# First attention of a two-layer block by pairs of heads: row tiles for the scores, outputs computed turned in column halves, bias and maximum in one instruction

## The chip, the cores and the metric

The kernel runs on one core of a Trainium2 chip. The metric is device time in microseconds (us) for one execution of the whole program, from a batch of 1 x 512 x 1024 activations to the result. Lower is better.

## The reference, cut to what matters

The program computes a first block (a mixing layer, an expert-choice layer, a gated layer) and then a second one (a gated MLP and a dilated attention). The change lies in the mixing layer of the first block: four pooling groups of 128 channels, and a neighbourhood attention of 8 heads of 64 channels over a grid of 8 rows by 64 columns. All rows are in reach; of the columns each query sees 16.

```python
z = rms_norm(x, norm_mix) @ w_in                    # 512 x 2048: u, q, k, v
y_pool = einsum(window_mean_g(u) - u, w_pool[g]) * pool_scale      # g = 0..3, windows 2, 4, 8, 16
q = rms_norm(q, q_norm) * HD ** -0.5;  k = rms_norm(k, k_norm)
s = einsum('bhcd,bhicjd->bhcij', q_r, k_nb) + rpb[:, dr, dc]       # within the column window
o = softmax(s) @ v_nb
x = x + concat([y_pool, o]) @ w_out
```

## The kernel before, in words

The program is written engine by engine, with semaphores, and each engine runs its own list in order. TensorE fills banks of PSUM (eight of them, 512 float32 a partition each); VectorE and ScalarE read them. A list `order`, made by `note`, says in which order TensorE fills banks and which engine frees each; fill number i takes bank i modulo 8, and `begin` waits until the fill eight places earlier has been read.

The projections `q`, `k` (turned, channels on partitions: `Q1`, `K1`, two heads of 64 partitions to a chunk of 128) and `v` (`V1`, tokens on partitions) stand in SBUF when the attention starts. There are 32 items, one for each query tile of 128 tokens and head (`ITEMS1`, head fastest, L337). The two outer query tiles need 256 keys, the two inner ones 384 (`KEYS1`), so there are 16 items of each width. Float32 matmuls are issued as two matmul records each.

For item j, the engines do this (loops at L843 on TensorE, L1236 on ScalarE, L1611 on VectorE):

- TensorE writes the mask of the column window into a bank (L849, bf16, one column wide per key) and adds the scores of one head to it (L850, 64 partitions deep).
- VectorE adds the relative position bias and writes `S1` (L1621), then takes the negated maximum over the row (L1624).
- ScalarE computes the exponential with the row sum (L1252, and a separate instruction that reads the sum).
- TensorE turns the probabilities of item j-2 in 128 x 128 pieces (L857), ScalarE copies them to `PT1` (L1244).
- TensorE multiplies the turned probabilities of item j-3, as the stationary operand, with `V1`, 64 columns wide (L864). VectorE scales the result by the reciprocal of the row sum (L1629, L1634) into `O1`, tokens on partitions.

Between items VectorE does 8 folds of 1 MB weight slabs (L1463, two instructions each) for the second block's modulation, at j = 2, 5, 8, ..., and TensorE sums one of the results at j = 12 (`ada_cols`, L817). GpSimd computes the pooling windows meanwhile (L708 to L722) into `pool_d`.

After the items TensorE does two 512-wide sums (`ada_rows`, L824), the four pooling matmuls (L874), and 16 transposes of `O1` (L879, fills `ot1`). ScalarE and VectorE split pooling results and attention outputs into a high and a low part (`BH`, `BL`; L1215, L1519, L1648), and TensorE starts `w_out` (L796 to L798), which needs chunk after chunk of them (`f_lo`). Then come norm, router, top-k, and 16 experts, whose weights arrive by DMA in a ring of 12 slabs.

Of the kernel before, what the change touches and what calls it, by code (L numbers as in the profile page):

```python
# [7 lines left out]
P = 128  # L8
D = 1024
KD = D // P  # L10
S = 512
# [68 lines left out]
def bass_kernel(nc, a, out):  # L80
# [8 lines left out]
    with ExitStack() as ctx:  # L89
# [31 lines left out]
        ACC1 = at("ada_acc1", 136, [P, D])  # L121
# [5 lines left out]
        DT = at("pool_d", 90, [P, 4, S])  # L127
# [3 lines left out]
        P1 = [at(f"p1_{i}", 105 + 1.5 * i, [P, 384]) for i in range(2)]  # L131
        PT1 = [at(f"pt1_{i}", 108 + 1.5 * i, [P, 384]) for i in range(2)]
        O1 = at("o1", 112 + 8, [P, NT, 512])
# [65 lines left out]
        RS = [st(38), st(39)]  # L199
        RR = [st(40), st(41)]  # L200
# [4 lines left out]
        SSV = st(112, 16)  # L205

# [94 lines left out]

        order, fills, count = [], {}, {"act": 0, "dve": 0, "lo": 0}
        ring0 = [0]

        def note(key, eng):
            count[eng] += 1
            fills[key] = (len(order), eng, count[eng], ring0[0])
            order.append(key)
# [14 lines left out]
        def note_attn(tag, n):  # L323
            for j in range(n + 3):
# [6 lines left out]
                if tag == "a1" and j == 12:  # L331
                    note(("ada", 1), "dve")
# [11 lines left out]
        ITEMS1 = [(t, h) for t in range(NT) for h in range(H1)]  # L344
        note_attn("a1", len(ITEMS1))
# [4 lines left out]
        for c in range(4):  # L350
            note(("ot1", c), "lo")
# [12 lines left out]
        N_BEFORE_E, ring0[0] = len(order), len(order)  # L364
        COUNT_BEFORE_E = dict(count)
        note_norm(2)
# [64 lines left out]
        def bank(key):  # L431
            i, _, _, r0 = fills[key]
            return PS[(i - r0) % 8]
# [26 lines left out]
        a_nm, a_exp, a_rr = sem("neg_max"), sem("exp_done"), sem("row_rec")  # L460
# [90 lines left out]
        def item1(j):  # L551
            tr, h = ITEMS1[j]
            t = NT - 1 - tr
            kts = KEYS1[t]
            return tr, t, h, kts, len(kts) * P
# [122 lines left out]
        def _(pool):  # L678
# [17 lines left out]
            for g in range(4):  # L696
# [22 lines left out]
                nc.gpsimd.tensor_tensor(DT[:, g, :], cur[:, 8:8 + S], CNT[:, :], ALU.mult).then_inc(p_step, 1)  # L719
                n += 1  # L720
                pool.wait_ge(p_step, n)
                nc.gpsimd.tensor_tensor(DT[:, g, :], DT[:, g, :], UP[:, g, 8:8 + S],  # L722
# [7 lines left out]
        def _(pe):  # L730
# [3 lines left out]
            def begin(key):  # L734

                assert order[at_fill[0]] == key, (order[at_fill[0]], key)
                at_fill[0] += 1
                i, _, _, r0 = fills[key]
                if i - r0 >= 8:
                    _, eng, n, _ = fills[order[i - 8]]  # L740
                    pe.wait_ge(freed[eng], n)
                return bank(key)
# [38 lines left out]
            def tm_unit(ws, keys, ah, al, f0=None):  # L781

                banks = []
                for s in range(2):
                    hi, lo = slab_ready(ws[s])
                    for t in range(NT):
# [3 lines left out]
                        for k in range(4):  # L790
                            kc = 4 * s + k
                            if f0 is not None and t == 0:
                                pe.wait_ge(f_lo, f0 + kc + 1)
# [49 lines left out]
            n_items = len(ITEMS1)  # L843
            for j in range(n_items + 3):
                if j < n_items:
                    tr, t, h, kts, n = item1(j)
                    rows = slice((h % 2) * HD1, (h % 2 + 1) * HD1)
                    b = begin(("a1s", j))
                    mm(b[:, 0:n], ident_bf, CW[:, WINC[t]:WINC[t] + n], start=True, stop=False)  # L849
                    mm(b[:, 0:n], Q1[rows, h // 2, tr * P:(tr + 1) * P],  # L850
                       K1[rows, h // 2, kts[0] * P:kts[0] * P + n], start=False, stop=True).then_inc(filled, 1)
                if 2 <= j < n_items + 2:
                    _, _, _, kts, n = item1(j - 2)
                    pe.wait_ge(a_exp, j - 1)
                    b = begin(("a1t", j - 2))
                    for i in range(len(kts)):
# [1070 lines left out]
```

## Time and profile before

| | us |
|---|---|
| median of 3 runs | 2204.75 |
| lowest, highest | 2201.35, 2206.04 |
| profiled execution, its own time | 2205.0 |
| its span in the trace | 2203.2 |
| TensorE busy | 2036.4 (92%) |
| VectorE busy | 926.9 (42%) |
| ScalarE busy | 568.2 (26%) |

The trace counts from the first instruction's start; the execution's time is 1.8 us more than the span. Busy time of TensorE is modelled from pipelined matmuls, so it says that the engine had work, not that it ran at its peak. The clock that TensorE was granted is shown by stretch, as a share of 2.4 GHz: 1.00 is 2.4 GHz and 0.50 is 1.2 GHz.

### The profile page before, as it was taken

What the parts mean: (1) busy time and instruction counts of PE and PEld (TensorE: products, weight loads), DVE (VectorE), ACT (ScalarE), POOL (GpSimd) and SP (SyncE); (2) the same over time, 40 slices, a digit from 0 to 9 for tenths busy, and PEclk for the clock granted to TensorE, in tenths of its full rate; (3) what the DMA queues carried; (4) which work ended last, traced back from release to release, by engine and by line L of the source; (5) the groups of instructions that cost most, each with busy time, mean ns of one, the idle gap of its engine ahead of it and who ended that gap; (6) DMA issues with size and microseconds to landing.
All of it is one profiled execution on the core that took longest, in us unless ns stands there. A gap on an engine that the chain in (4) does not pass through costs nothing.

```text
span 2203.2 us, 24215 instructions
## 1 busy us (share of the span) xinstructions
PE 2036.4 (92%) x9141; PEld 1209.9 (55%) x9141; DVE 926.9 (42%) x1483; ACT 568.2 (26%) x980; POOL 37.7 (2%) x40
## 2 busy tenths in 40 slices
PE   7999979999999999999999888999999998989798
PEld 6756753332222222222222276888888786867687
DVE  4866451111111111111111165366455758696963
ACT  4333341111001001110011134442232544553510
POOL 1050000000000000000000000000000000000000
PEclk9965889999999999999999988999999998989899
DMA  8441249999999999999999933545243122011010
GB/s 264 139 139 39 103 174 404 422 422 422 422 422 422 422 422 422 422 422 422 422 422 422 415 126 119 194 138 179 93 156 115 60 93 77 20 58 58 20 39 39
DMA packets 132041, 528.15 MB, mean 240 GB/s; under 512 B 9862, under 2 KB 55748, under 8 KB 82692
## 3 DMA queue, kind: packets, MB, share of 16 engines
q1 hardware_dynamic: 129348, 520.55, 60.0%
q0 software_dynamic: 1008, 3.52, 0.7%
q10 hardware_dynamic: 1616, 3.15, 0.4%
q8 instruction: 45, 0.74, 0.1%
q14 instruction: 24, 0.20, 0.0%
HBM read 524.95 MB, written 2.23 MB: 239 GB/s over the span
## 4 chain that ended last, share of the span: by engine, by line
PE 55%; DMA 33%; DVE 7%; ACT 2%; issue 1%; SPq 1%; ACTq 0%; DVEq 0%
DMA w_expert<-in_w_gate 16%; DMA w_expert<-in_w_up 15%; PE bank L776 7%; PE bank L777 7%; PE bank L778 7%; PE bank L963 6%; PE bank L796 5%; PE bank L797 5%; PE bank L798 5%; PE bank L850 2%; PE bank L808 1%; PE bank L864 1%; PE bank L973 1%; DMA raw<-in_w_ple_gate 1%; SPq L630 1%
## 5 line engine op out<-in xcount | busy, mean ns | idle before, releaser
L963 PE MATMUL bank<-w_expert,chosen 128*64 128x512 f32 x2048 | 483.7, 602 | 62.5 <-DMA w_expert<-in_w_up 46.2
L963 PEld LDWEIGHTS bank<-w_expert,chosen 128*64 128x64 f32 x2048 | 130.3, 136 | 396.0 <-issue 232.7
L1710 DVE TENSOR_TENSOR x_res<-x_res,bank 128x512 f32<-128x512 f32 x136 | 87.3, 683 | 428.6 <-PE bank L982 408.3
L776 PE MATMUL bank<-act_hi,w_hi 128*128 128x512 f32 x608 | 248.5, 409 | 0.1
L1473 DVE TENSOR_TENSOR w_lo<-raw,w_hi 128x2048 fp32r<-128x2048 f32 x75 | 171.9, 2292 | 167.2 <-ACT w_hi L1180 167.2
L778 PE MATMUL bank<-act_hi,w_lo 128*128 128x512 f32 x608 | 237.6, 391 | 0.0
L777 PE MATMUL bank<-act_lo,w_hi 128*128 128x512 f32 x608 | 237.6, 391 | 0.0
L973 PE MATMUL bank<-w_expert,hidden_t 128*64 128x512 f32 x1024 | 229.9, 596 | 6.0 <-ACT hidden_t L1332 4.6
L1180 ACT CAST w_hi<-raw 128x2048 fp32r<-128x2048 f32 x75 | 142.9, 1905 | 169.4 <-PE bank L798 163.2
L1732 DVE TENSOR_TENSOR hidden_rows<-gate_silu,bank 128x512 f32<-128x512 f32 x32 | 20.6, 684 | 364.5 <-PE bank L963 364.5
L1535 DVE RECIPROCAL full<-full 128x512 f32<-128x512 f32 x38 | 127.3, 3350 | 64.0 <-ACT full L1234 63.9
L973 PEld LDWEIGHTS bank<-w_expert,hidden_t 128*64 128x64 f32 x1024 | 74.6, 137 | 138.8 <-issue 121.1
L776 PEld LDWEIGHTS bank<-act_hi,w_hi 128*128 128x128 f32 x608 | 114.7, 189 | 28.9 <-issue 5.5
L777 PEld LDWEIGHTS bank<-act_lo,w_hi 128*128 128x128 f32 x608 | 114.7, 189 | 28.2 <-issue 5.5
L778 PEld LDWEIGHTS bank<-act_hi,w_lo 128*128 128x128 f32 x608 | 114.5, 188 | 24.3
L796 PE MATMUL bank<-w_hi,mix_hi 128*128 128x512 f32 x256 | 100.4, 392 | 0.0
L798 PE MATMUL bank<-w_hi,mix_lo 128*128 128x512 f32 x256 | 99.7, 389 | 0.0
L797 PE MATMUL bank<-w_lo,mix_hi 128*128 128x512 f32 x256 | 99.6, 389 | 0.0
L1326 ACT ACTIVATE gate_silu<-bank 128x512 f32<-128x512 f32 x32 | 17.4, 594 | 289.2 <-PE bank L963 289.2
L796 PE MATMUL bank<-w_hi,act_hi 128*128 128x512 f32 x224 | 89.1, 398 | 2.2 <-ACT full L1202 2.2
L797 PE MATMUL bank<-w_lo,act_hi 128*128 128x512 f32 x224 | 88.4, 395 | 0.0
L798 PE MATMUL bank<-w_hi,act_lo 128*128 128x512 f32 x224 | 88.1, 393 | 0.0
(255 smaller groups left out, 2450.4 us busy)
## 6 DMA issues: line engine op xcount, KB each, us to landing
w_expert<-in_w_gate SPq DMA_DIRECT2D x128, 1024.0 KB, 24.9
w_expert<-in_w_up SPq DMA_DIRECT2D x128, 1024.0 KB, 26.5
w_expert<-in_w_down SPq DMA_DIRECT2D x128, 1024.0 KB, 26.2
raw<-in_a_w_in SPq DMA_DIRECT2D x24, 1024.0 KB, 5.7
raw<-in_b_w_in SPq DMA_DIRECT2D x16, 1024.0 KB, 5.3
raw<-in_a_ada_w SPq DMA_DIRECT2D x12, 1024.0 KB, 5.2
raw<-in_b_ada_w SPq DMA_DIRECT2D x12, 1024.0 KB, 5.8
raw<-in_kv_ada_w SPq DMA_DIRECT2D x8, 1024.0 KB, 5.2
```

Source lines behind the costliest of these rows:

```text
L776: mm(b[:, :], hi[:, cols], ah[:, kc, :], start=(kc == 0), stop=False)
L777: mm(b[:, :], hi[:, cols], al[:, kc, :], start=False, stop=False)
L778: last = mm(b[:, :], lo[:, cols], ah[:, kc, :], start=False, stop=(kc == KD - 1))
L796: mm(b[:, :], a_hi, hi[:, r], start=(kc == 0), stop=False)
L797: mm(b[:, :], a_hi, lo[:, r], start=False, stop=False)
L798: last = mm(b[:, :], a_lo, hi[:, r], start=False, stop=(kc == KD - 1))
L963: last = mm(PS[b0 + n][HALF[x], :], XE[:, k % 4, HALF[k // 4]], WE[place][:, r], start=(k == 0), stop=(k == KD - 1), skip_group_check=True)
L973: last = mm(PS[4][HALF[x], :], HT[:, 2 * q + k, HALF[half]], WE[place][:, r], start=(i == 0 and k == 0), stop=(i == 7 and k == 1), skip_gr ...
L1180: nc.scalar.copy(WHI[w % 2][:, :], RAW[slot(n)][:, :]).then_inc(hi_ready, 1)
L1473: tt(WLO[w % 2][:, :], RAW[slot(n_of["W"][w])][:, :], WHI[w % 2][:, :].bitcast(F32), ALU.subtract).then_inc(lo_ready, 1)
L1535: nc.vector.reciprocal(r, r).then_inc(h_rec, 1)
L1710: tt(part, part, ps[:, :], ALU.add).then_inc(d_add, 1)
```

## The change

The 32 items become 16 pairs: pair i is one chunk of two heads and one query tile (`ITEMS1`, tile fastest). TensorE opens two banks, writes the mask into each, and then computes the two heads' scores, one from partitions 0 to 63 and one from 64 to 127. The outputs are computed turned: `V1` (64 columns of one head) is the stationary operand and `PT1` (128 columns) the moving one, and the two heads of a pair write the lower and the upper 64 partitions of one bank, which collects all four query tiles of a chunk. The bank then holds what the 16 transposes of `O1` gave, so these and `O1` go. Since a query is now a column of the output, the reciprocal of the row sum is applied before the transposes, by VectorE, to the probabilities (L1662, 256 or 384 wide, in place). Bias, negation and minimum are one instruction of VectorE (`tensor_tensor_reduce`, L1675), which is issued with a second small one that writes the accumulated column; the exponential takes scale -1. Each pair's output column chunk is split into `BH`, `BL` inside the attention loop, at i = 6, 10, 14 and after the loop. The folds lie at i = 1 to 4 and 8 to 11, `ada_cols` at i = 8. Banks are now given by hand: scores 0 to 3, transposes 4 and 5, outputs 6 and 7. The pooling result goes to `u_padded` in place of `pool_d`. `w_out` waits for the pooling chunks only (`f_chunks`), in its first half.

```diff
+        ITEMS1 = [(c, t) for c in range(H1 // 2) for t in range(NT)]
...
+            for i in range(N1 + 2):
+                if i == 8:
                     ada_cols(1, ACC1)
+                if i < N1:
+                    c, tr, t, kts, n = item1(i)
+                    banks = [begin(("a1s", i, x)) for x in range(2)]
+                    for b in banks:
+                        mm(b[:, 0:n], ident_bf, CW[:, WINC[t]:WINC[t] + n], start=True, stop=False)
+                    for x, b in enumerate(banks):
+                        rows = slice(x * HD1, (x + 1) * HD1)
+                        mm(b[:, 0:n], Q1[rows, c, tr * P:(tr + 1) * P],
+                           K1[rows, c, kts[0] * P:kts[0] * P + n], start=False, stop=True).then_inc(filled, 1)
+                if i >= 2:
+                    c, tr, t, kts, n = item1(i - 2)
+                    pe.wait_ge(freed["act"], fills[("a1t", i - 2, 1)][2])
+                    b = begin(("ot1", c), ends_next=False) if tr == 0 else bank(("ot1", c))
+                    for k, kt in enumerate(kts):
+                        for x in range(2):
+                            last = mm(b[x * HD1:(x + 1) * HD1, tr * P:(tr + 1) * P],
+                                      V1[:, kt, (2 * c + x) * HD1:(2 * c + x + 1) * HD1],
+                                      PT1[2 * (i % 2) + x][:, k * P:(k + 1) * P], start=(k == 0), stop=(k == len(kts) - 1),
+                                      skip_group_check=True)
...
+                if 1 <= i <= N1:
+                    c, tr, t, kts, n = item1(i - 1)
+                    for x in range(2):
+                        slot_ = 2 * ((i - 1) % 2) + x
+                        pe.wait_ge(a_nrm, 2 * (i - 1) + x + 1)
+                        b = begin(("a1t", i - 1, x))
+                        for k in range(len(kts)):
+                            last = nc.tensor.transpose(b[:, k * P:(k + 1) * P], P1[slot_][:, k * P:(k + 1) * P], ident)
+                        last.then_inc(filled, 1)
...
-            for c in range(4):
-                b = begin(("ot1", c))
-                for t in range(NT):
-                    last = nc.tensor.transpose(b[:, t * P:(t + 1) * P], O1[:, t, c * P:(c + 1) * P], ident)
-                last.then_inc(filled, 1)
...
+            def attention1():
+                for i in range(N1 + 1):
+                    if i < N1:
+                        n = item1(i)[4]
+                        for x in range(2):
+                            j = 2 * i + x
+                            act.wait_ge(freed["dve"], fills[("a1s", i, x)][2])
+                            if i >= 2:
+                                act.wait_ge(filled, fill_no(("a1t", i - 2, x)))
+                            nc.scalar.activation(P1[j % 4][:, 0:n], S1[x][:, 0:n], ACT.Exp, bias=NM[x], scale=-1.0,
+                                                 accum_out=RS[j % 4]).then_inc(a_exp, 1)
...
+                    if i >= 6 and i % NT == 2:
+                        ot1_hi(i // NT - 1)
...
+            def probabilities(j):
+                n, p = item1(j // 2)[4], P1[j % 4]
+                dve.wait_ge(a_exp, j + 1)
+                nc.vector.reciprocal(RR[j % 4], RS[j % 4]).then_inc(a_rr, 1)
+                dve.wait_ge(a_rr, j + 1)
+                ts(p[:, 0:n], p[:, 0:n], RR[j % 4], None, ALU.mult).then_inc(a_nrm, 1)
+
+            for i in range(N1 + 1):
+                if i == 8:
                     ada_out(1)
+                for x in range(2):
+                    if i < N1:
+                        c, tr, t, kts, n = item1(i)
+                        h = 2 * c + x
+                        b = take(("a1s", i, x))
+                        if i:
+                            dve.wait_ge(a_exp, 2 * (i - 1) + x + 1)
...
+                        nc.vector.tensor_tensor_reduce(
+                            S1[x][:, 0:n].rearrange("p (j k) -> p j k", k=ROWS),
+                            b[:, 0:n].rearrange("p (j k) -> p j k", k=ROWS), bias, -1.0, 3e38, ALU.add, ALU.min, NM[x]
+                            ).then_inc(freed["dve"], 1)
+                    if i >= 1:
+                        probabilities(2 * (i - 1) + x)
+                if i in (1, 2, 3, 4, 8, 9, 10, 11):
+                    fold(len(folded))
+                if i >= 6 and i % NT == 2:
+                    ot1_lo(i // NT - 1)
+            ot1_lo(3)
```

TensorE's list, before, in the middle of the attention, for one item of 256 keys: mask, scores, two transposes, two output matmuls.

```order
L849 MATMUL bank<-const_wins 128x256 [waits bank_read_by_dve]
L850 MATMUL bank<-k_84,q_83 128x256
L857 MATMUL bank<-const_early,p_1_99 128x128 [waits bank_read_by_act,exp_done]
L857 MATMUL bank<-const_early,p_1_99 128x128
L864 MATMUL bank<-v_85,pt_0_100 128x64 [waits bank_read_by_dve,bank_read_by_act]
L864 MATMUL bank<-v_85,pt_0_100 128x64
```

TensorE's list, of the change, for one pair of 256 keys; the outputs belong to the pair two places earlier and the transposes to the one before.

```order
L868 MATMUL bank<-const_wins 128x256 [waits bank_read_by_dve]
L868 MATMUL bank<-const_wins 128x256
L871 MATMUL bank<-k_84,q_83 128x256 x2
L879 MATMUL bank<-pt_0_101,v_85 64x128 [waits bank_read_by_act]
L879 MATMUL bank<-pt_1_102,v_85 64x128
L879 MATMUL bank<-pt_0_101,v_85 64x128
L879 MATMUL bank<-pt_1_102,v_85 64x128
L879 MATMUL bank<-pt_0_101,v_85 64x128
L879 MATMUL bank<-pt_1_102,v_85 64x128
L893 MATMUL bank<-const_early,p_2_99 128x128 [waits bank_read_by_act,probabilities]
L893 MATMUL bank<-const_early,p_2_99 128x128
L893 MATMUL bank<-const_early,p_3_100 128x128 [waits bank_read_by_act,probabilities]
L893 MATMUL bank<-const_early,p_3_100 128x128
```

The transposes used to wait for the exponential; they now wait for `probabilities`, which VectorE signals after its scaling, once for each head.

VectorE's list, before, for one item: bias, maximum, reciprocal and scaling of earlier items.

```order
L1621 TENSOR_TENSOR s_0_96<-bank,bias_master 128x384 [waits exp_done,bank_filled]
L1624 TENSOR_REDUCE stats<-s_0_96 128x1 [waits bank_read_by_dve]
L1629 RECIPROCAL stats<-stats 128x1 [waits bank_read_by_dve,exp_done]
L1634 TENSOR_SCALAR o_102<-bank,stats 128x64 [waits row_rec,bank_filled]
```

VectorE's list, of the change, for one pair (`ISA` is the fused instruction, with its small second one).

```order
L1675 ISA s_0_95,stats<-bank,bias_master 128x384 [waits exp_done,bank_filled]
L1675 ISA stats 128x1
L1660 RECIPROCAL stats<-stats 128x1 [waits exp_done]
L1662 TENSOR_SCALAR p_2_99<-p_2_99,stats 128x384 [waits row_rec]
L1675 ISA s_1_96,stats<-bank,bias_master 128x384 [waits exp_done,bank_filled]
L1675 ISA stats 128x1
L1660 RECIPROCAL stats<-stats 128x1 [waits exp_done]
L1662 TENSOR_SCALAR p_3_100<-p_3_100,stats 128x384 [waits row_rec]
```

The scaling of pair i-1 stands behind the fused instruction of pair i, head by head, and that one waits for the scores of pair i.

## Rows read from the trace of the kernel before

**Rows 1.** The page: busy time of TensorE, and its granted clock in 40 slices.

```profile
PE 2036.4 (92%) x9141; PEld 1209.9 (55%) x9141; DVE 926.9 (42%) x1483; ACT 568.2 (26%) x980; POOL 37.7 (2%) x40
...
PEclk9965889999999999999999988999999998989899
```

**Rows 2.** Stretches: length; busy (and count) of PE, PEld, DVE, ACT, POOL; PEclk, DMA share, GB/s.

```profile
200.00:220.00 20.00, 20.00 (x69) 13.44 (x69) 11.23 (x27) 6.69 (x20) 0.00 (x0) 0.50 0.00 0
...
235.00:240.00 5.00, 5.00 (x26) 3.23 (x25) 3.48 (x7) 2.93 (x5) 0.00 (x0) 1.00 0.11 15
```

**Rows 3.** Waits from 118 to 235 us: total us, times, longest us.

```profile
PE bank L857 <- ACT p L1252: 4.5, 3, 3.2
```

**Rows 4.** Timeline of one item of 256 keys: start us, us, instruction.

```profile
219.29 0.42 PE L849 MATMUL bank<-const_wins 128*128 128x256 bf16 x1
...
219.64 1.22 PE L850 MATMUL bank<-k,q 64*128 64x256 f32 x2
...
220.90 0.60 DVE L1621 TENSOR_TENSOR s<-bank,bias_master 128x256 f32<-128x256 f32 x1 [1.08 <-PE bank L850]
...
222.01 0.42 PE L849 MATMUL bank<-const_wins 128*128 128x256 bf16 x1
```

**Rows 5.** Timeline, the scores of two successive items of 384 keys.

```profile
165.41 1.65 PE L850 MATMUL bank<-k,q 64*128 64x384 f32 x2
...
169.31 1.65 PE L850 MATMUL bank<-k,q 64*128 64x384 f32 x2
```

**Rows 6.** Timeline of the first item, at the granted clock of 1.00.

```profile
118.54 0.27 PE L849 MATMUL bank<-const_wins 128*128 128x256 bf16 x1 [0.88 <-ACT v L1276]
...
118.74 0.70 PE L850 MATMUL bank<-k,q 64*128 64x256 f32 x2
```

**Rows 7.** Groups by line and shape, 118 to 235 us: count, busy us, mean ns, idle before.

```profile
L1463 DVE SCALAR_TENSOR_TENSOR ada_acc<-raw,stats,ada_acc 128x1024 f32<-128x1024 f32 x14 | 21.5, 1533 | 9.3 <-PE bank L850 9.0
...
L1621 DVE TENSOR_TENSOR s<-bank,bias_master 128x384 f32<-128x384 f32 x16 | 13.4, 835 | 6.6 <-PE bank L850 6.6
...
L1621 DVE TENSOR_TENSOR s<-bank,bias_master 128x256 f32<-128x256 f32 x16 | 9.7, 604 | 7.5 <-PE bank L850 7.5
...
L1624 DVE TENSOR_REDUCE stats<-s 128x1 f32<-128x256 f32 x16 | 6.7, 420 | 0.6
...
L1252 ACT ACTIVATION_READ_ACCUMULATOR p<-s,stats 128x1 f32 x32 | 6.0, 186 | 0.0
...
L1629 DVE RECIPROCAL stats<-stats 128x1 f32<-128x1 f32 x32 | 4.9, 154 | 0.2
```

**Rows 8.** Two lines that scale by a column: ns min/median/max, first and last start.

```profile
L1886 DVE TENSOR_SCALAR diag<-const_early,negmax x96: 273/279/289, 2092.9 to 2146.6; 128x128 f32<-128x128 f32 x96
...
L1460 DVE TENSOR_SCALAR ada_acc<-raw,stats x8: 741/748/1166, 25.5 to 1579.3; 128x1024 f32<-128x1024 f32 x8
```

**Rows 9.** Timeline in an expert: column halves (L963), row halves (L982), at clock 1.00.

```profile
735.03 1.13 PE L982 MATMUL bank<-expert_out,sel_gated_t 64*128 64x512 f32 x4
736.09 1.94 PE L963 MATMUL bank<-w_expert,chosen 128*64 128x512 f32 x8
...
739.02 5.37 PE L963 MATMUL bank<-w_expert,chosen 128*64 128x512 f32 x24
```

**Rows 10.** Stretches at the start of a later attention, columns as in rows 2.

```profile
1962.50:1965.00 2.50, 2.50 (x14) 2.50 (x14) 1.98 (x8) 1.75 (x7) 0.00 (x0) 0.50 0.81 286
1965.00:1967.50 2.50, 2.50 (x19) 2.26 (x18) 2.26 (x11) 2.06 (x10) 0.00 (x0) 0.95 0.03 7
```

**Rows 11.** Timeline behind the attention.

```profile
237.88 1.91 PE L879 MATMUL bank<-const_early,o 128*128 128x128 f32 x16
...
239.54 0.48 PE L796 MATMUL bank<-w_hi,mix_hi 128*128 128x512 f32 x1
...
239.82 3.85 ACT L1215 ACTIVATE mix_hi<-bank 128x512 fp32r<-128x512 f32 x4 [1.05 <-PE bank L879]
...
240.95 4.02 DVE L1648 TENSOR_TENSOR mix_lo<-bank,mix_hi 128x512 fp32r<-128x512 f32 x4 [1.40 <-ACT mix_hi L1215]
```

More of the change, by code:

```diff
@@ L205, in bass_kernel @@
         SSV = st(112, 16)
+        RS = [st(128 + i) for i in range(4)]
+        RR = [st(132 + i) for i in range(4)]
         def pcol(name, k=0, n=1):
@@ L302, in bass_kernel, with note @@
         order, fills, count = [], {}, {"act": 0, "dve": 0, "lo": 0}
-        ring0 = [0]
-        def note(key, eng):
+        ring, holder = [0], {}
+        def note(key, eng, at_bank=None):
             count[eng] += 1
-            fills[key] = (len(order), eng, count[eng], ring0[0])
+            if at_bank is None:
+                at_bank = ring[0]
+                ring[0] = (at_bank + 1) % 8
+            fills[key] = (len(order), eng, count[eng], at_bank, holder.get(at_bank))
+            holder[at_bank] = key
             order.append(key)
@@ L732, in _, with begin, ends @@
             at_fill = [0]
-            def begin(key):
+            def begin(key, ends_next=True):
+                if ends_next:
+                    ends(key)
+                before_ = fills[key][4]
+                if before_ is not None:
+                    pe.wait_ge(freed[fills[before_][1]], fills[before_][2])
+                return bank(key)
+            def ends(key):
                 assert order[at_fill[0]] == key, (order[at_fill[0]], key)
                 at_fill[0] += 1
[L738 to L742, printed above, removed]
             def norm(k):
@@ L791, in tm_unit @@
                             kc = 4 * s + k
-                            if f0 is not None and t == 0:
+                            if f0 is not None and t == 0 and kc < f_chunks:
                                 pe.wait_ge(f_lo, f0 + kc + 1)
@@ new lines, in ot1_lo @@
+            def ot1_lo(c):
+                assert fills[("ot1", c)][2] == f[0] + 1
+                dve.wait_ge(f_hi, f[0] + 1)
+                hi, lo = (x[:, 4 + c, :].rearrange("p (r c) -> p c r", r=ROWS) for x in (BH, BL))
+                tt(lo, from_grid(bank(("ot1", c))[:, :]), hi.bitcast(F32), ALU.subtract).then_inc(f_lo, 1)
+                f[0] += 1
+            def probabilities(j):
[4 more added lines that the diff above has]
+                ts(p[:, 0:n], p[:, 0:n], RR[j % 4], None, ALU.mult).then_inc(a_nrm, 1)
```

133 lines of the change are left out of this document (43 added, 90 removed).

## The prediction

> **What bounds the kernel now.** I read the page first. TensorE has work for 92% of the span, and its granted clock is full nearly everywhere but in the fourth slice, where it is five tenths [rows 1]. The stretches put a place to that: from 200 to 220 us TensorE is busy for all of the 20 us at a clock of 0.50, which is 1.2 GHz, and just behind the attention it is at 1.00 again [rows 2]. So the first attention is bound by TensorE at the lower of its two levels. The waits agree: in the 117 us of the stage TensorE waits 4.5 us for the exponential, in 3 places [rows 3], and the bias, the fold and the output scaling on VectorE wait for TensorE, not the reverse [rows 4, 7]. All that follows (w_out, router, top-k, the experts' weights, whose slabs are asked for as earlier ones are used) starts from the attention's end, so I count a microsecond there as one in the total.
>
> An item of 256 keys takes 222.01 - 219.29 = 2.72 us [rows 4], one of 384 keys 169.31 - 165.41 = 3.90 us [rows 5]. Four pairs of the new kernel (one chunk of two heads, all tiles: two pairs of 256 and two of 384) are eight such items: 4 x 2.72 + 4 x 3.90 = **26.5 us**. There are four such chunks.
>
> **The new loop.** The change puts a ring in place of a pipeline. The transposes of pair i-1 wait for VectorE's scaling of pair i-1, which stands behind the fused instruction of pair i, which waits for the scores of pair i, which stand behind the transposes of pair i-2. One turn of the ring is:
>
> 1. From the first mask to VectorE's first instruction. Before: mask to scores 0.35 us, scores to the bias 220.90 - 219.64 = 1.26 us [rows 4]. Now a second mask is in between, 256 columns at 1.2 GHz, 0.21. Sum 1.82 us. For 384 keys the two masks are 0.11 longer each and the scores (four cycles a column) 0.43: 2.47 us. The second head's scores run on behind and are not waited for.
> 2. Two fused instructions. The trace has none. I take the addition it contains, 0.60 and 0.84 us [rows 7], plus 0.10 for the small second instruction. Bounds: nothing for it, and ScalarE's 0.19 for its own read of a sum [rows 7]; from above also addition plus maximum as now, 0.60 + 0.42. I take the addition because it reads the same bank and the same strided bias. 0.70 and 0.94 each.
> 3. Two reciprocals (0.15 [rows 7]) and two scalings in place. The scaling lies between 0.28 us for 128 columns and 0.75 for 1024 [rows 8]: 0.35 and 0.42 on the line between them. 0.50 and 0.57 together.
> 4. From the last scaling to the next mask: about 0.2 us of signal, the second head's transposes, 2 or 3 of 0.21 us at this clock, 0.1 to the mask: 0.73 and 0.94.
>
> The widths in a chunk run 256, 384, 384, 256. Pair by pair (fused of this pair, scaling and transposes of the one before, lead of the next): 1.4 + 1.0 + 0.73 + 2.47 = 5.6; 1.88 + 1.0 + 0.73 + 2.47 = 6.1; 1.88 + 1.14 + 0.94 + 1.82 = 5.8; 1.4 + 1.14 + 0.94 + 1.82 = 5.3. Sum **22.8 us** against 26.5, and over four chunks **-14.8 us**.
>
> TensorE's own work must fit into that turn. The halves matter here. At 1.2 GHz a pair of 256 keys then needs some 0.56 + 1.28 (scores) + 0.3 (change-over, as between scores and transposes now) + 1.1 to 1.2 (outputs) + 0.95 (transposes) = 4.2 us, one of 384 keys 5.8 us. That is 5.0 on average under a ring of 5.7: TensorE is close behind, and what it saves is not all collected. VectorE's ring is late next.
>
> **Other terms.**
> - Folds: two instructions of 1.28 us, 2.57 us, at eight places. They lie where VectorE otherwise waits for terms 4 and 1 (2.8 to 3.2 us), so the late four cost nothing. While GpSimd pools, they are slower: 14 of them sum to 21.5 us, not 18 [rows 7]. I add **+2**. Were the cover gone (the higher clock), they would cost about 1 us each.
> - The split of a finished output chunk inside the loop: VectorE waits for transposes, ScalarE's copies (about 0.5), ScalarE's high part (3.85 / 4 = 0.96) and then needs 1.0 itself [rows 11]: some 3.6 us after the last scaling, where 2.8 were free. Three times: **+2.5**.
> - Filling and draining with longer turns: **+1**.
> - `ada_cols`: the same 16 small matmuls, moved, not changed: 0. ScalarE does the same exponentials and copies, and scale -1 costs nothing; it has over half its time free [rows 2]. Masks are still one for each head. GpSimd's pooling in place has as many instructions and ends long before it is needed: 0. SP's loads wait for the same folds at the same share of the loop: 0.
> - Behind the attention: the 16 transposes of `O1` go. `w_out` starts at 239.54, and the transposes stood from 237.88 [rows 11]: **-1.65**. The pooling chunks are split by then, or the last within the time of the first matmuls; the attention chunks were split earlier.
>
> Sum: -14.8 + 2 + 2.5 + 1 - 1.65 = **-11 us**. The profiled execution took 2205.0 us, 0.25 over the median of 2204.75, so this gives **2194 us**.
>
> **A rule against the change.** The row first: going from row halves to column halves and back in the experts costs nothing that I can see, 1.06 us for four records being two and a half times 0.43 [rows 9], and I add 0.3 only once in each pair. The Trainium skill (TensorEngine Tiling, Key Properties) says that changing the tiling mode drains the engine. By it a pair would have three such changes (full, rows, columns, full), where two items have four now. If each cost 0.3 us, TensorE's turn would be 4.8 and 6.4 us, 5.6 on average and about the ring's own length, and the total some 2 us higher.
>
> **The rivals.**
> - *The clock comes up.* For it: a later attention starts at 0.50, is busy without a gap, and goes to 0.95 in the next stretch [rows 10]; the new loop has matmul columns flowing for about 79% of a turn where now it is some 72%. Against it: the stage has stayed at 0.50 with TensorE always busy [rows 2], and at the higher clock the same work fills only half of a turn, so that it may fall again. At 1.00 throughout: mask to scores is 0.20 us [rows 6], lead 1.15 and 1.47, term 4 0.51 and 0.62, a chunk 18.4 us, -32.6 for four; folds now stick out, +8; output splits +4.4; +1; `ada_cols` and the 512-wide sums run faster, -3.5; -1.65. Sum -24: **2181 us**; up for half of the time, 2187. [...]
> - *The halves do not overlap here*, since the matmuls are 128 to 384 columns wide and not 512, and each waits for its weights. Then scores cost four records in a row and outputs eight or twelve: 5.3 and 7.6 us a pair, 25.8 a chunk. -2.8 in all, the folds and splits hidden, -1.65: **2200 us**. Rows 9 speak against it.
> - *The fused instruction is slow*, and the change ends slower. It is in the ring twice for each pair, 32 times in all, with nothing to hide it. If it makes a pass for the addition and one as long for the minimum, it takes 1.2 and 1.7 us, 0.6 and 0.8 more than I took: 32 x 0.7 = +22, and **2216 us**. It decides from 11 / 32 = 0.35 us over my price. For it: addition and maximum now take 0.60 and 0.42 us apart [rows 7]. Against: ScalarE's exponential sums in the same pass for 0.19 more.
>
> **How the numbers follow.** Forecast (clock stays at 0.50) 45%, the clock comes up for a part or all 30%, no overlap 15%, slow fused instruction 10%. About 0.2%, 4.4 us, is what a measurement of this kernel can tell from no change. The range runs from the full clock, 2180, to 2203, above the case without overlap with some of the unpriced waits; it leaves out the slow instruction. Faster: the first two and half of the third, 0.82. Same: 0.1. Slower: 0.08.
>
> **What would show it.** In the profile after: the attention ends about 10 us earlier; two successive masks of pairs are 5.3 to 6.1 us apart; TensorE waits before the transposes (L893), for VectorE's scaling; granted clock 0.50; the four score records of 256 keys take 1.3 us and eight output records 1.1 to 1.2 us; the fused instruction 0.6 and 0.84 us. I am wrong on the ring if TensorE does not wait there, on the halves if these records take 1.7 us, on the clock if the stage shows over 0.50.

## The result and the profile after

The changed kernel takes 2179.65 us, median of four runs (2173.96 to 2181.42), beside 2204.96 us for the kernel before on the same chip: a ratio of 0.9893, 95% interval [0.9874, 0.9911]. It is 25 us faster where 11 were forecast, and 0.35 us below the low end of the range. The profiled execution, the slowest of the four, took 2181.42 us, its span is 2179.6 (before: 2203.2, so -23.6 by the trace).

The page of the changed kernel, against [rows 1]:

```profile
PE 1993.5 (91%) x9125; PEld 1175.5 (54%) x9125; DVE 917.6 (42%) x1483; ACT 567.4 (26%) x980; POOL 38.8 (2%) x40
...
PEclk9967999999999999999999998999999998989899
```

TensorE has 43 us less of busy time, of which 24 show in the span: the rest has turned into waits. The fourth slice stands at seven tenths of the clock, where it was five.

Stretches of the changed kernel, with the columns of [rows 2] (length; busy and count of PE, PEld, DVE, ACT, POOL; granted clock, DMA share, GB/s):

```profile
152.65:158.53 5.88, 5.08 (x22) 2.51 (x21) 2.60 (x8) 2.15 (x6) 0.00 (x0) 0.50 0.19 79
...
160.00:180.00 20.00, 17.59 (x90) 10.95 (x88) 13.13 (x34) 6.11 (x19) 0.00 (x0) 0.59 0.16 53
180.00:200.00 20.00, 13.48 (x88) 7.48 (x87) 15.86 (x42) 9.87 (x27) 0.00 (x0) 0.84 0.16 54
...
118.50:205.00 86.50, 64.19 (x322) 35.70 (x322) 65.11 (x141) 35.81 (x93) 29.00 (x23) 0.64 0.31 101
```

TensorE, which was busy for every one of 20 us at 0.50 in [rows 2], is now busy for 64 of 86.5 us and at 0.64 on average. The clock is at 1.00 up to about 125 us, at 0.50 from 126 to 172 us, and goes up and down afterwards.

The waits from 118 to 225 us of the changed kernel (total us, times, longest us), against [rows 3]:

```profile
ACT p L1269 <- DVE stats L1675: 45.8, 31, 5.0
PEld bank L893 <- DVE p L1662: 33.5, 30, 5.2
PE bank L893 <- DVE p L1662: 23.2, 27, 4.6
DVE mix_lo L1654 <- ACT mix_hi L1235: 10.4, 3, 5.5
...
DVE s L1675 <- PE bank L871: 8.7, 5, 3.0
```

This is the ring that the forecast described: before its transposes (L893) TensorE waits for VectorE's scaling in 27 places. VectorE waits for scores in only five; elsewhere a fold or a split mostly fills that time. It also waits three times for ScalarE's part of an output split, but only two of these waits (2.45 us each) lie in the loop. The third stands behind it, and the split at i = 10 finds its input ready, behind a fold:

```profile
160.22 1.05 DVE L1654 TENSOR_TENSOR mix_lo<-bank,mix_hi 128x512 fp32r<-128x512 f32 x1 [2.45 <-ACT mix_hi L1235]
...
184.28 1.01 DVE L1654 TENSOR_TENSOR mix_lo<-bank,mix_hi 128x512 fp32r<-128x512 f32 x1
...
213.03 1.03 DVE L1654 TENSOR_TENSOR mix_lo<-bank,mix_hi 128x512 fp32r<-128x512 f32 x1 [5.54 <-ACT mix_hi L1235]
```

**Where the 23.6 us came from.** Four marks on TensorE, from the timelines:

| mark | before | after | difference, added since the mark above | forecast |
|---|---|---|---|---|
| `ada_rows` begins (attention's end) | 230.67 | 211.85 | -18.8 | -9.3 |
| `w_out` begins | 239.54 | 218.04 | -2.7 | -1.65 |
| first expert matmul | 326.51 | 303.24 | -1.8 | 0 |
| end of the span | 2203.2 | 2179.6 | -0.3 | 0 |

The third row is no work of the change. In the kernel before, the transposes of the router's norm fell into a low clock (0.52 from 289.2 to 292.4 us):

```profile
289.20 3.20 PE L755 MATMUL bank<-const_early,x_norm 128*128 128x128 f32 x14 [0.94 <-DVE x_norm L1492]
```

The same fourteen in the changed kernel, at 1.00:

```profile
268.03 1.75 PE L773 MATMUL bank<-const_early,x_norm 128*128 128x128 f32 x14 [0.94 <-DVE x_norm L1531]
```

1.45 of the 1.8 us are there. From `w_out` to the experts the kernels below take 83.0 to 85.9 us, the kernel before 87.0.

**One turn of the ring, with nothing else in it.** Timeline of the changed kernel from one pair of 384 keys to the next mask (start us, us, instruction):

```profile
152.65 0.84 PE L868 MATMUL bank<-const_wins 128*128 128x384 bf16 x2
...
153.43 1.65 PE L871 MATMUL bank<-k,q 64*128 64x384 f32 x4
155.01 1.12 PE L879 MATMUL bank<-pt,v 128*64 128x128 f32 x8
155.11 0.83 DVE L1675 CUSTOM_DVE_ANT_1 s<-bank,bias_master 128x384 f32<-128x384 f32 x1 [3.00 <-PE bank L871]
155.87 0.08 DVE L1675 DVE_READ_ACCUMULATOR2_ANT stats<- 128x1 f32 x1
155.87 0.16 DVE L1660 RECIPROCAL stats<-stats 128x1 f32<-128x1 f32 x1
...
156.06 0.42 DVE L1662 TENSOR_SCALAR p<-p,stats 128x384 f32<-128x384 f32 x1
156.40 0.84 DVE L1675 CUSTOM_DVE_ANT_1 s<-bank,bias_master 128x384 f32<-128x384 f32 x1
...
157.35 0.42 DVE L1662 TENSOR_SCALAR p<-p,stats 128x384 f32<-128x384 f32 x1
...
157.83 0.90 PE L893 MATMUL bank<-const_early,p 128*128 128x128 f32 x3 [0.39 <-DVE p L1662]
...
158.53 0.64 PE L868 MATMUL bank<-const_wins 128*128 128x256 bf16 x2
```

Mask to VectorE's start: 155.11 - 152.65 = 2.46 us (priced 2.47). The two heads on VectorE: 157.77 - 155.11 = 2.66 us (priced 1.88 + 1.14 = 3.02). Last scaling to the next mask: 158.53 - 157.77 = 0.76 us (priced 0.94). The turn is 5.88 us where the same pieces were priced at 6.43, at the same clock of 0.50. The small second instruction has 0.08 us and begins 0.76 us after its parent's start, at the same moment as the reciprocal: it costs nothing of its own. The signal from the scaling's end to the transposes is 157.83 - 157.77 = 0.06 us, not 0.2.

Groups by line and shape of the changed kernel, 118 to 225 us (count, busy us, mean ns, idle before), against [rows 7]:

```profile
L1502 DVE SCALAR_TENSOR_TENSOR ada_acc<-raw,stats,ada_acc 128x1024 f32<-128x1024 f32 x14 | 22.3, 1592 | 0.3
...
L1675 DVE CUSTOM_DVE_ANT_1 s<-bank,bias_master 128x384 f32<-128x384 f32 x16 | 13.4, 838 | 8.0 <-PE bank L871 7.5 <-ACT p L1269 0.2
...
L1675 DVE CUSTOM_DVE_ANT_1 s<-bank,bias_master 128x256 f32<-128x256 f32 x16 | 9.6, 604 | 1.3 <-PE bank L871 1.2
...
L1662 DVE TENSOR_SCALAR p<-p,stats 128x384 f32<-128x384 f32 x16 | 6.9, 433 | 0.6
L1662 DVE TENSOR_SCALAR p<-p,stats 128x256 f32<-128x256 f32 x16 | 6.8, 426 | 0.6
```

The fused instruction takes 838 and 604 ns, the addition alone took 835 and 604 [rows 7]: the minimum is free. The folds take about as long in all as they did (22.3 us, before 21.5).

**The turns beside each other.** The first masks of five pairs, from TensorE's timeline:

```profile
127.91 0.84 PE L868 MATMUL bank<-const_wins 128*128 128x384 bf16 x2
...
167.42 0.59 PE L868 MATMUL bank<-const_wins 128*128 128x256 bf16 x2
...
192.39 0.49 PE L868 MATMUL bank<-const_wins 128*128 128x384 bf16 x2
...
196.62 0.49 PE L868 MATMUL bank<-const_wins 128*128 128x384 bf16 x2
...
201.71 0.64 PE L868 MATMUL bank<-const_wins 128*128 128x256 bf16 x2
```

The turn from 192.39 to 196.62 took 4.23 us at a clock of 1.00. The one from 196.62 to 201.71 has the same widths as the turn shown above, took 5.09 us where that one took 5.88, and began at the higher clock (0.78 for its first 1.6 us). The six turns from 127.91 to 164.15, where `ada_cols` begins, lie at 0.50 throughout.

### The profile page after: what moved, and what is told of

Read it like the earlier page. It is cut to its first block, busy times and chain, and to the rows that moved or that the text cites. A ratio compares the mean times of both kernels' runs of the same rounds, so it can differ in the third digit from the quotient of the medians.

```text
span 2179.6 us, 24073 instructions
## 1 busy us (share of the span) xinstructions
PE 1993.5 (91%) x9125; PEld 1175.5 (54%) x9125; DVE 917.6 (42%) x1483; ACT 567.4 (26%) x980; POOL 38.8 (2%) x40
## 4 chain that ended last, share of the span: by engine, by line
PE 52%; DMA 33%; DVE 9%; issue 2%; ACT 2%; SPq 1%; DVEq 0%; ACTq 0%
DMA w_expert<-in_w_gate 16%; DMA w_expert<-in_w_up 15%; PE bank L794 7%; PE bank L795 7%; PE bank L796 7%; PE bank L983 6%; PE bank L814 5%; PE bank L816 5%; PE bank L815 5%; PE bank L826 1%; PE bank L993 1%; DMA raw<-in_w_ple_gate 1%; PE bank L1175 1%; DVE s L1675 1%; SPq L643 1%
## 5 line engine op out<-in xcount | busy, mean ns | idle before, releaser
L1365 ACT ACTIVATE gate_silu<-bank 128x512 f32<-128x512 f32 x32 | 17.4, 594 | 289.2 <-PE bank L983 289.2
```

## The experiments

Twelve runs on three chips, each beside the kernel before on its chip (medians there: 2202.52 for e1 to e4, 2204.72 for e0 and e5 to e7, and 2200.42 us for e7 again and e8 to e10). Ratios are to it. "Mark" is the start of `ada_rows` in the one execution that was profiled; it is 211.85 us in the changed kernel's first profile. The diffs are against the changed kernel unless another is named.

**e0, the changed kernel again.**

> The changed kernel itself, so that the others of this batch are compared on one chip: 0.989 of the kernel before, as measured first.

2179.59 us, ratio 0.9892 [0.9874, 0.9909]. Mark at 210.48 us, mean clock 0.76 from 118.5 to 205 us where the first profile shows 0.64. So the clock of one kernel differs between executions, and 0.12 of it goes with 1.4 us.

**e1, the addition and the maximum apart.**

```
-  nc.vector.tensor_tensor_reduce(
-      S1[x][:, 0:n].rearrange("p (j k) -> p j k", k=ROWS),
-      b[:, 0:n].rearrange("p (j k) -> p j k", k=ROWS), bias, -1.0, 3e38, ALU.add, ALU.min, NM[x]
-      ).then_inc(freed["dve"], 1)
+  tt(S1[x][:, 0:n].rearrange("p (j k) -> p j k", k=ROWS),
+     b[:, 0:n].rearrange("p (j k) -> p j k", k=ROWS), bias, ALU.add).then_inc(s_added, 1)
+  dve.wait_ge(s_added, 2 * i + x + 1)
+  nc.vector.tensor_reduce(NM[x], S1[x][:, 0:n], AX.X, ALU.max, negate=True).then_inc(freed["dve"], 1)
...
-  nc.scalar.activation(P1[j % 4][:, 0:n], S1[x][:, 0:n], ACT.Exp, bias=NM[x], scale=-1.0,
+  nc.scalar.activation(P1[j % 4][:, 0:n], S1[x][:, 0:n], ACT.Exp, bias=NM[x],
```

> The fused instruction is taken apart again: an addition, then a negated maximum, everything else as in the changed kernel. Theory A (a ring through VectorE sets the length of a pair's turn): the fused one measures 0.60 and 0.84 us plus 0.08; apart it is 0.60 + 0.42 and 0.84 + 0.55, so 0.34 us more for 256 keys and 0.47 for 384, twice for each pair and with nothing to hide it: 16 x 0.34 + 16 x 0.47 = +13 us, 2193 us. Theory B (the gain comes from TensorE's own shorter work in halves, and VectorE is mostly hidden): under +4 us.

2199.94 us (2196.54 to 2201.45), ratio 0.9985 [0.9975, 0.9996]. The mark is at 226.74 us, 14.9 later than in the changed kernel's first profile. Groups of e1, 118 to 230 us, columns as above:

```profile
L894 PE MATMUL bank<-const_early,p 128*128 128x128 f32 x80 | 22.5, 401 | 37.2 <-DVE p L1663 36.9
...
L1679 DVE TENSOR_REDUCE stats<-s 128x1 f32<-128x384 f32 x16 | 8.8, 553 | 0.6
...
L1679 DVE TENSOR_REDUCE stats<-s 128x1 f32<-128x256 f32 x16 | 6.7, 420 | 0.6
```

The maxima are 15.5 us of VectorE's time; TensorE's wait for the scaling grows by 13.7 (23.2 to 36.9, at a mean clock of 0.64 and 0.63), and the mark moves by 14.9 (16.3 from e0's): all of it lies on the path. So VectorE's instructions in the ring count one for one, and without the fusion nearly nothing of the 25 us is left in the run time. (By the ratios the difference from e0 is 20 us, by the spans 15 to 17. The profiled execution of e1 was the fastest of its ten, 2196.54 us, 3.4 below their median, which accounts for most of that.)

**e2, outputs head by head** (all key tiles of one head, then of the other), so that the column halves do not alternate.

```
-  for k, kt in enumerate(kts):
-      for x in range(2):
+  for x in range(2):
+      for k, kt in enumerate(kts):
```

> The output matmuls of a pair are issued head by head instead of alternating, so that the two column halves run side by side only where the one head ends and the other begins. Output matmuls of a pair should go from 1.1 us (8 records, low clock) to about 1.7 and from 1.5 to 2.4. Theory A (ring through VectorE; TensorE waits 23 us in the attention before its transposes): the longer outputs end inside that wait, 0 to +5 us in all. Theory B (TensorE's own work sets the turn): +0.6 and +0.9 us a pair at the low clock, about +10 us.

2180.70 us, ratio 0.990 [0.988, 0.992]; mark 213.27. Timeline of e2, two groups at a clock of 0.50:

```profile
154.31 1.13 PE L879 MATMUL bank<-pt,v 128*64 128x128 f32 x8
...
168.03 2.03 PE L879 MATMUL bank<-pt,v 128*64 128x128 f32 x12
```

The twelve records of 384 keys take 2.03 us at 0.50 where the changed kernel's take 1.55; the eight of 256 keys take the 1.1 us that they took. Why only the twelve suffer is open. At the clock of 1.00 a group of twelve takes 1.15 us, not 0.88. The run times do not tell it from the changed kernel, and the mark is 1.4 to 2.8 us later. The eight groups of twelve lose about 3.0 us in all (four at the lower clock, four at the higher), so only a part of it, between nearly nothing and half, falls into TensorE's wait for the scaling. In this profile the stage from `w_out` to the experts is also 2.2 us shorter than in the changed kernel's (83.0 against 85.2), which the edit does not touch and which hides such a loss in the span.

**e3, each head's mask right before its scores**, so that the row halves cannot run together.

```
-  for b in banks:
-      mm(b[:, 0:n], ident_bf, CW[:, WINC[t]:WINC[t] + n], start=True, stop=False)
   for x, b in enumerate(banks):
+      mm(b[:, 0:n], ident_bf, CW[:, WINC[t]:WINC[t] + n], start=True, stop=False)
```

> Mask and scores of the first head, then mask and scores of the second, so the two row halves are never side by side; the first head's scores are ready one mask earlier (0.21 or 0.32 us at the low clock), the second's later by about a score record. Theory A (ring, in which only the first head's scores are waited for): -0.2 to -0.3 us a turn where the ring is not broken by a fold, up to -4 us in all, unless the second head's scores now come too late for VectorE. Theory B (the overlap of the row halves is a source of the gain): +0.4 and +0.6 us a pair, +6 to +10 us.

2182.70 us, ratio 0.9918 [0.9889, 0.9947]; mark 213.30. Timeline of e3, TensorE and VectorE in one pair of 384 keys:

```profile
153.49 1.65 PE L870 MATMUL bank<-k,q 64*128 64x384 f32 x2
155.07 0.50 PE L868 MATMUL bank<-const_wins 128*128 128x384 bf16 x1
155.17 0.84 DVE L1674 CUSTOM_DVE_ANT_1 s<-bank,bias_master 128x384 f32<-128x384 f32 x1 [2.67 <-PE bank L870]
155.50 1.64 PE L870 MATMUL bank<-k,q 64*128 64x384 f32 x2
...
157.18 0.83 DVE L1674 CUSTOM_DVE_ANT_1 s<-bank,bias_master 128x384 f32<-128x384 f32 x1 [0.63 <-PE bank L870]
```

One head's two records hold TensorE from 153.49 to 155.07, 1.58 us; in the changed kernel the four records of both heads take 155.01 - 153.43 = 1.58 us as well. The second head is free there: the overlap is complete, and I had priced half of it. Still the intervals overlap with e0's, and the mark is only 1.4 to 2.8 us later, though TensorE is busy for 75.75 us from 118.5 to 205 us where it was 64.19, both at a mean clock of 0.64. Its wait for the scaling takes that up: it falls from 23.2 to 12.4 us. VectorE starts earlier on the first head (155.17 - 153.04 = 2.13 us behind the first mask, not 2.46) and waits 0.63 us for the second. The one pays for half of the other.

**e4, filler matmuls for the clock.** Twelve matmuls of 128 columns in bfloat16 for each pair, into a part of a bank that nobody reads; the output's computation is unchanged.

```
+  for _ in range(4 if x else 8):
+      mm(PS[4 + x][:, 384:512], ident_bf, CW[:, 0:P], start=True, stop=True)
```

> Twelve small bf16 matmuls of 128 columns are added for each pair, into unused columns of the transposes' banks: 8 before the first head's wait, 4 before the second's. They compute nothing that is used. They are 1.3 us of work a pair at 1.2 GHz. Theory C (the granted clock follows how little TensorE pauses, and the second half of the attention gained because it came up there): the clock of the attention goes up, to 0.8 or more from the first turns on, and the time falls by 3 to 8 us in spite of the added work. Theory A without the clock: no gain, and +2 to +8 us from work that does not fit into the waits.

2177.28 us (2175.7 to 2180.45), ratio 0.9885 [0.9863, 0.9907]. Stretches of e4, columns as above:

```profile
118.50:205.00 86.50, 65.26 (x523) 41.70 (x522) 67.27 (x150) 37.33 (x99) 28.40 (x22) 0.85 0.31 101
```

The clock is at 0.85 and the mark at 207.61, 2.9 to 4.2 us earlier than in the two profiles of the changed kernel, with 192 matmuls more. By the run times it is 2 us, inside the interval. So the clock is worth something in the ring, but 0.2 of it little more than 4 us, with the fillers' own time in that figure.

**e5, scores one pair ahead.** The scores of pair i+1 are issued before the transposes of pair i-1; VectorE's `ada_out` goes one pair later.

```
+  scores(0)
   for i in range(N1 + 2):
...
-      if i < N1:
...
+      if i + 1 < N1:
+          scores(i + 1)
```

> The ring is opened: TensorE issues the scores of pair i+1 before it waits for the scaled probabilities of pair i-1, so VectorE finds its next scores ready. The read of ada_cols' result moves behind the fused instructions of pair 8. Theory A (the wait of VectorE for TensorE and of TensorE for VectorE, in turn, sets the length): VectorE's own work is 0.53 + 0.08 + 0.15 + 0.35 = 1.1 us a head for 256 keys and 1.4 for 384, so 16 pairs take 40 us, with folds (20 us and more) and splits (4) 65 to 70; TensorE has 4.2 and 5.8 us a pair at the low clock (80 us), 45 at the high one. The attention ends 8 to 20 us earlier than in the changed kernel: 2160 to 2172 us. Theory B (TensorE's own work): under 2 us.

2171.30 us (2168.39 to 2174.26), ratio 0.9847 [0.9831, 0.9862]; mark 202.19, 8.3 to 9.7 us earlier than in the changed kernel. TensorE's wait for the scaling is 20.4 us from 118.5 to 205 us. VectorE no longer waits for scores, but it still waits 11.8 us, in three places, for the high part of an output split: 3.8 and 2.1 us in the loop and 5.9 behind it.

**e6, the low part of an output split one pair later on VectorE.**

```
-  if i >= 6 and i % NT == 2:
+  if i >= 7 and i % NT == 3:
       ot1_lo(i // NT - 1)
```

> VectorE's part of the split of a finished output chunk stands one pair later, when ScalarE's part is long done. In the changed kernel VectorE waits 2.45 us for it in two of three places. Theory A: the wait goes and the subtraction of 1.0 us falls into the time in which VectorE waits for scores: 1.5 to 2.5 us less at two or three places, -3 to -6 us, 2174 to 2177 us. If TensorE's transposes and scores took as long as that wait anyway: no change.

2178.15 us, ratio 0.9877 [0.9862, 0.9892]; mark 208.88. The wait for the high part is nearly gone inside the loop, but the wait for scores rises from 8.7 us in 5 places to 15.5 in 9. Alone it gains 1.4 us by the median of its chip, within the interval, and 1.6 to 3.0 us at the mark: where the split no longer holds VectorE up, VectorE waits for scores.

**e7, both.**

> Both: scores one pair ahead and the low parts one pair later. Theory A: with the ring open the wait for ScalarE's part would be all of what stops VectorE, so the two add up: -12 to -25 us against the changed kernel, 2155 to 2168 us.

2160.81 us (2158.89 to 2162.95), ratio 0.9802 [0.9787, 0.9817]; mark 192.84. That is 19 us more than the change alone, where the two edits gave 8 and 1.5. With the scores already there, VectorE has nothing to wait for but the split's high part, and e6 takes that wait away: what is left of it is 5.0 us in two places.

**e7 again, and what bounds it.**

> The kernel of e7 once more, on the chip of e8 to e10, to compare with: 2159 to 2163 us. If its attention shows another mean granted clock than 0.80 while the total stays within 1 us, VectorE sets its turn and not the clock.

2160.61 us, ratio 0.9812 [0.9793, 0.9832]; mark 192.71, and the mean clock is 0.80 in both, so this pair cannot tell the clock's part. A stretch of it does name the bound:

```profile
125.00:155.00 30.00, 21.46 (x104) 11.56 (x102) 29.46 (x56) 11.43 (x34) 24.23 (x19) 0.57 0.62 195
```

VectorE is busy for 29.46 of 30 us there, beside GpSimd's pooling. Behind it, from 155 to 192 us, it is busy for 32.9 of 37 us, and what bounds that part is not shown.

**e8, e7 with the second head's scaling on ScalarE.**

```
+  def scaled(i):
+      j, m = 2 * i + 1, item1(i)[4]
+      act.wait_ge(a_rr, j + 1)
+      nc.scalar.activation(P1[j % 4][:, 0:m], P1[j % 4][:, 0:m], ACT.Identity, scale=RR[j % 4]).then_inc(a_nrm1, 1)
```

It stands between the two exponentials of the next pair; VectorE takes the reciprocal ahead of the second fused instruction.

> The earlier scores and the later split of e7, and besides the second head of each pair has its probabilities scaled by ScalarE (about 0.5 us) while VectorE does the next addition and maximum. VectorE loses 0.42 us a pair and waits for less; ScalarE gains about 0.6 us a pair, and its copies of turned probabilities come that much later. Theory A (in e7 the attention is bound by VectorE, busy 98% from 125 to 155 us): up to 16 x 0.3 = 5 us less than e7, about 2156. Theory B (the ring in e7 runs through ScalarE's exponentials and copies as well, or TensorE's columns bind): no gain, or up to 3 us more than e7, 2160 to 2164.

2155.41 us (2152.84 to 2159.19), ratio 0.9796 [0.9776, 0.9816]; mark 187.91, 4.8 us before e7's. The same stretch of e8:

```profile
125.00:155.00 30.00, 22.81 (x133) 13.55 (x133) 28.35 (x56) 16.49 (x46) 24.05 (x18) 0.72 0.55 182
```

The gain is that of theory A: 5.2 us by the medians of one chip, 4.8 at the mark. The interval overlaps that of e7 on the same chip, so the run times alone do not tell the two apart; e7's two marks lie within 0.13 us of each other. (The span of e8's profile is 8.2 us shorter than e7's, but 3.4 of that lie behind the mark.) **e8 has the lowest time here**, about 1% below the changed kernel by the ratios (0.9796 to 0.9892).

**e9, e7 with six fillers a pair** (the edit of e4 with four and two).

> e7 with six idle matmuls of 128 columns in bfloat16 before the transposes of each pair (four and two), which change nothing in the output. Theory A (TensorE's granted clock still costs time in the attention of e7, mean 0.80): the clock rises to about 0.9 and the total falls by 1 to 3 us against e7. Theory B (VectorE sets the turn in e7 and TensorE has slack): total the same within 1 us, whatever the clock; and where TensorE is at 0.50 the added columns cost 0.1 us each at the most.

2161.96 us, ratio 0.9825 [0.9807, 0.9843]; mark 195.95, mean clock 0.80 again. No gain: the mark is 3.1 us later than e7's, and the median 1.4 us higher on the same chip, a little over the 1 us that theory B allowed. The premise of theory A, a higher clock, did not come about, so that the run does not test what a higher clock would bring e7; it shows that fillers without it cost time.

**e10, the changed kernel with the second head's scaling on ScalarE.**

> The changed kernel with the second head's scaling moved to ScalarE, its order otherwise as it is. In the changed kernel the ring runs over both scalings and VectorE stands behind the scores. Theory A (ring: score, addition, reciprocal, scaling, transposes): the last scaling now starts when the second reciprocal is done, beside the second addition of 0.84 or 0.60 us, so that the ring is about 0.3 to 0.5 us shorter in each of 16 pairs: 5 to 8 us less, about 2173. Theory B (ScalarE's exponential of the first head and its accumulator read stand before the scaling, which then ends no earlier than VectorE's did): within 1.5 us of the changed kernel.

2171.79 us (2169.13 to 2176.07), ratio 0.9865 [0.9844, 0.9887]; mark 203.71, 6.8 to 8.1 us before the changed kernel's two. Theory A: a scaling taken out of VectorE's row in the ring shortens each of the 16 turns by 0.4 to 0.5 us, about its own length (0.35 and 0.42). The two kernels ran on different chips; by the ratios to the kernel before (0.9865 and 0.9892) the gain is 6 us.

## Why the prediction was right and wrong

**Right.** The direction and the mechanism: the pipeline bound by TensorE at 1.2 GHz became a ring through VectorE. TensorE waits at the line that was named, the fused instruction costs what its addition costs, and e1 shows that VectorE's part of the ring is path microsecond for microsecond. Mask to VectorE's first instruction was priced to 0.01 us in the turn shown. The rival of a slow fused instruction is refuted by 838 and 604 ns.

**Wrong: steps 2 and 4 of the ring were priced too high.** For the small second instruction I added 0.10 us to each fused one, between bounds of nothing and 0.42. It runs beside its parent's end: nothing was the right bound. With the smaller steps from one VectorE instruction to the next, its row of a pair is 0.36 us shorter at 384 keys, and at 256 keys 192.05 - 189.97 = 2.08 against 2.40 (the turn that begins at 188.15). In step 4 the signal is 0.06 us, not 0.2, and the last transposes to the mask take 0.70. Together 0.5 us a turn; over 16 turns that is an estimated **-8 us**, carried over from the two turns read here, and the largest part of the 12.6 us by which the spans differ more than was forecast (23.6 against 11). The bound of nothing stood in the text but was not carried into the range: a term that enters 32 times needs its bounds carried 32 times, which takes another 3.2 us off the 2181 of the full clock and puts the low end near 2177.5.

**Wrong: the clock.** "Clock stays at 0.50" had 45%. It was at 0.64 on average (and 0.76 in e0). After its fall at 126 us it first rises again at about 173 us, behind a stretch from 164 to 172 us in which TensorE was busy for 7.94 of 8 us. That does not explain the rise: in the kernel before it was busy without a gap from 140 to 230 us and stayed at 0.50 ([rows 2] shows 20 us of it), and in e0 the clock is back at 1.00 at 131 us already. What brings it up is open. The clock gave less than its rival had it. Of the attention's -18.8 us the forecast has -9.3, the cheaper steps -8, and folds and splits cost some 2 us more than priced (below); what is left for the clock is about -3.5. Two turns show most of it: the one from 192.39 us took 4.23 us at 1.00 where the same pieces at 0.50 are 2.46 + 2.53 + 0.53 = 5.52, and the one from 196.62 us took 5.09 where its like at 0.50 took 5.88. e0 and e4, whose marks lie 1 to 2 us lower for each 0.1 of clock above the first profile's, agree. The rival summed full-clock turns, with folds sticking out; at 0.64 both are partial. That its 2181 us lies within 1.4 us of the measured time is luck: the clock was at 1.00 for few of the turns, and most of the miss is that of the steps, which the rival priced as the forecast did.

**Errors that cancelled.** In the six turns from 127.91 to 164.15 us, all at 0.50, the forecast's prices come to 34.5 us for the ring and 37.3 with its folds and first split; they took 36.2. The steps were 3 us too dear there and the folds nearly 2 us too cheap. From 167.42 to 201.71 us, seven turns, the prices come to 41.9 us and the trace has 34.3: there the folds lie under the wait, as foreseen, and the steps and the clock both save.

**Wrong: nothing behind the attention.** `w_out` starts 1.05 us earlier than the removed transposes explain: the matmuls ahead of it (6.19 us, before 7.21) ran at a mean clock of 0.78 where it was 0.72. Another 1.8 us come from a dip of the clock that the router's transposes no longer meet. I had put both at zero without a bound; a stage that is only shifted can meet another clock.

**The halves.** TensorE's own work of a pair was priced at 4.2 and 5.8 us, 5.0 on average. It is a little under that: TensorE is busy for 5.08 us of the turn shown and for 4.8 on average over the four turns from 139.33 to 164.15 us. The split is another: both heads' scores cost two slots and not three, and some 0.3 us stand around them: 1.58 us for 384 columns, where four cycles a column at 1.2 GHz are 1.28, and 159.09 to 160.25, 1.16 us, for 256 columns where they are 0.85. The Trainium skill (TensorEngine Tiling, Key Properties) says that changing the mode drains the engine; 0.3 us by the scores is the most that this trace can have of it, against the three times 0.3 of the estimate, and no run here separates it from other causes. Neither this nor the overlap was worth much time here by itself. e3 undoes the overlap of the row halves, e2 that of the column halves for the pairs of 384 keys, and each loses 1.4 to 2.8 us at the mark, nothing that the run times resolve, since TensorE had slack in the ring. No run undoes both; the prediction's 5.3 and 7.6 us a pair without any overlap, 6.45 on average, would be longer than the turns measured (5.4 on average over thirteen, `ada_cols` left out), so that the two halves together may well have been needed. That is argued and not shown.

**The folds and splits**, priced at +2 and +2.5, can be read from the timelines: by how much VectorE's first fused instruction of a pair starts later than 1.77 us (256 keys) or 2.46 us (384 keys) behind the pair's first mask, which is what it takes where nothing else holds it up. Beside GpSimd's pooling the folds hold it up by 0.6, 1.8 and 1.2 us:

```profile
142.92 0.59 DVE L1675 CUSTOM_DVE_ANT_1 s<-bank,bias_master 128x256 f32<-128x256 f32 x1
...
149.41 0.83 DVE L1675 CUSTOM_DVE_ANT_1 s<-bank,bias_master 128x384 f32<-128x384 f32 x1
```

(The pairs' masks stand at 139.33 and 145.75 us.) That is 3.6 us and not 2; the late folds cost nothing by themselves. The splits cost 0.9, 1.1 (behind a fold) and 0.9 us, 2.9 in all, against 2.5, though by two waits and not three. e6, which hides most of them, gains 1.6 to 3.0 us at the mark.

## What to carry to other kernels

Once a loop is a ring through two engines, price each hop from the nearest pair of rows, carry the bounds of each small term by the number of turns, and expect the ring to take microseconds one for one (e1, e10) while the other engine's savings count for little (e2, e3). Break such a ring by issuing the next scores before the dependent step, and look at once for what the freed engine waits for next: the two edits of e7 are worth 19 us together and 9 to 10 apart. When an engine is busy for 98% of a stretch, move one of its equal pieces to a neighbour that is busy for 38% (e8).

## What the runs showed of the hardware

- The fused addition and minimum over 128x384 and 128x256 float32 takes 838 and 604 ns, as the plain addition; its read of the accumulator (0.08 us) runs beside the next small instruction. ScalarE's own such read is 0.19 us long, and the copy behind it starts 0.09 us after it does (152.09 and 152.18 us), which is when the exponential itself ends.
- Two heads' float32 scores in row halves take the time of one (1.58 us both, for 384 keys at 1.2 GHz).
- Two folds of 128x1024 take 2.60 us alone and 4.35 and 4.50 beside GpSimd's pooling.
- From the end of a VectorE instruction to a waiting transpose: 0.06 us (157.77 to 157.83).
- The granted clock of the same kernel over the same stretch was 0.64 in one execution and 0.76 in another; the run times do not show it beyond their scatter.
